# Spare TensorE products of 320 columns, and a shorter chain of VectorE instructions from router logits to gather

## The chip, the cores and the metric

The kernel runs on one core of a Trainium2 chip. The metric is the device time of one execution in microseconds (us), as the median of several runs. A core has a matrix engine (TensorE, in the rows PE, with PEld for its weight loads), VectorE (DVE), ScalarE (ACT), GpSimd (POOL) and a queue engine that issues transfers (SP). They run side by side and meet at semaphores.

## The reference, cut to what matters

Two transformer blocks on 256 tokens of 1024 values, all in float32.

```python
# first block, two layers
for l in range(2):
    x = x + hybrid_mixer(rms_norm(x, norm_mix[l]), ...)
    h = rms_norm(x, norm_ffn[l])
    x = x + (swiglu(h, ...) if l == 0 else moe_swiglu(h, ...))
x = rms_norm(x, norm_final)
# moe_swiglu: 8 experts of width 2816, the two best of each token
logits = h @ router
top_vals, top_idx = top_k(logits, 2); gates = softmax(top_vals)
out = sum over e of gate[:, e] * swiglu(h, wg[e], wu[e], wd[e])
# second block
x = x + attention and short convolution, gated, through w_o
h2 = rms_norm(x)
# hierarchical_moe: the best of 4 groups, then the two best of its 4 experts (width 256)
g = top_1(softmax(h2 @ w_rg + b_rg)); e = top_2(softmax(logits of the experts in the group))
x = x + sum over the chosen of gate * expert(h2)
x = x + sigmoid(rms_norm(x) @ w_pg) * (p @ w_ple)
```

## The kernel before, in words

Each engine has a program of its own, written out by hand in the order of the work (`block.tensor`, `block.vector` and so on), and waits for the others at semaphores; there is no planner. The precision of float32 is kept with two parts: a number is split into a high part in the type fp32r and a low part, the rest, and each product is made three times (high by high, high by low, low by high: `three`, L1033 to L1035).

Weights come as tiles of 1 MB, 128x2048 numbers, into a ring of six slots (`ring`), in one fixed order. For each tile ScalarE writes the high part (`high`, L668; in the expert stages L804), VectorE the low part (`low`, `rest_of`, L1524) into one of three places, and TensorE uses both. SP issues the next transfer into a slot (L500) once the low part of the tile in it is made.

**The norm turns.** `norm(n)` stands on ScalarE and VectorE, `turn(n)` on TensorE. ScalarE squares the first 128 tokens (L676) and so signals `sumsq_ready`, VectorE squares the other 128 (L1537), GpSimd takes the inverse root (L603), VectorE scales both halves (L1548), TensorE turns them in sixteen 128x128 transposes (L1017), ScalarE writes the high part (L684), VectorE the low part (L1524). `norm` on VectorE can be given a weight tile to split after that (`tile`). From `sumsq_ready` on TensorE runs `spare(0, 12)`, twelve 128x128 transposes of the identity into PSUM bank 0 (L1006), whose results nobody reads; the turn after `norm(4)` doesn't exist, since `norm(4)` is not turned.

**The routes.** `route(...)` on TensorE makes the logits with 32 small products (`small_rows`, L1206 and L1207: 16 or 8 columns, in the second block 40 or 20), waits for `exps_wanted`, runs twelve spare transposes into bank 4, waits for `mask_ready`, makes the ranks (ten products, L1220 to L1224), that is for each token and chosen expert how many tokens before it chose the same, and runs sixteen more. On VectorE `route` (first block, L1735 to L1755) and `route2` (second, L1761 to L1791) take the logits, ask ScalarE for the exponentials, find each logit's place among its peers (`places`, L1719 to L1723: five instructions that compare all pairs; `route2` calls it once for the groups and once for the experts of each of four groups), set the mask (L1741; L1772), and make the gates meanwhile. After the ranks they write `table`: for each of three passes (`PASSES`: 96 token slots per expert and pass) three or four instructions. Then comes `over_flag` (L1727 to L1729), three instructions that tell whether any expert has more than 96 tokens, and then the low part of a weight tile.

**The sweep.** `sweeps` waits for the flag's semaphore and calls `sweep`; `choose` copies an expert's row of the table (L1796) and writes the picks, 0/1 matrices of tokens by slots (L1799, L1802). TensorE gathers the chosen tokens with them (`gather_half`, 16 products at L1233 and one transpose at L1235 per half), ScalarE and VectorE split the gathered tokens, and the products of the first expert begin (L1033). After all experts each engine reads the flag and repeats the sweep for the further passes if it is set.

Of the kernel before, what the change touches and what calls it, by code (L numbers as in the profile page):

```python
# [8 lines left out]
ALU = mybir.AluOpType  # L9
# [3 lines left out]
P = 128  # L13
S = 256
TT = S // P
# [3 lines left out]
HALF = 512  # L19
# [6 lines left out]
EXPERTS = 8  # L26
# [3 lines left out]
GROUPS2 = 4  # L30
CAP = 96
PASSES = -(-S // CAP)
# [69 lines left out]
def build(nc, A, out):  # L102
    ctx = ExitStack()
    with ctx:
# [26 lines left out]
        work = sb("work", [P, 5, D])  # L131
# [57 lines left out]
        den = sb("den", [P, 2 + 8])  # L189
        pair_gt, pair_eq = (work[:, 3, k * P:(k + 1) * P] for k in range(2))  # L190
        ntab = (PASSES * EXPERTS) + 1
# [808 lines left out]
        def _(pe):  # L1000
            mm = nc.tensor.matmul

            def spare(b, n):

                for k in range(n):
                    nc.tensor.transpose(PS[:, b, (k % 4) * P:(k % 4 + 1) * P], ident[:], ident[:])  # L1006

            def turn(n):

                if n:  # L1010
                    pe.wait_ge(sumsq_ready, n + 1)
                    spare(0, 12)
                for t in range(TT):
                    pe.wait_ge(norm_applied, 2 * n + t + 1)
                    for b in range(2):
                        for c in range(4):
                            last = nc.tensor.transpose(PS[:, 2 * t + b, c * P:(c + 1) * P],  # L1017
                                                       h[:, t, (4 * b + c) * P:(4 * b + c + 1) * P], ident[:])
                        last.then_inc(h_turned, 1)
# [191 lines left out]
            def route(n, pair, ne, groups, k):  # L1211
# [4 lines left out]
                pe.wait_ge(exps_wanted, k)  # L1216
                spare(4, 12)
                pe.wait_ge(mask_ready, k)
# [5 lines left out]
                mm(PS[:, 1, 2 * groups:3 * groups], ones[:], m[1], start=False, stop=True).then_inc(rank_ready, 1)  # L1224
                spare(4, 16)

# [264 lines left out]
            pe.wait_ge(conv_gated, 2)  # L1491
            spare(4, 8)
            for m in range(4):
# [12 lines left out]
        def _(v):  # L1506
# [224 lines left out]
            def route():  # L1731
# [18 lines left out]
                rank = PS[:, 1, 0:TT * EXPERTS].rearrange("p (t e) -> p e t", t=TT)  # L1750
                for p in range(PASSES):
                    c = slice(p * EXPERTS, (p + 1) * EXPERTS)
                    own.mark(ts(table[:, c, 0, :], rank, float(-p * CAP), None, ALU.add))
                    own.mark(copy(table[:, c, 1, :], m8.rearrange("p t e -> p e t")))
                    own.mark(copy(table[:, c, 2, :], e8.rearrange("p t e -> p e t")))  # L1755
                over_flag(1, EXPERTS)

            def route2():
# [9 lines left out]
                   ALU.subtract).then_inc(exps_wanted, 1)  # L1768
                for g in range(5):
                    places(lg[:, :, 4 * g:4 * g + 4], TT, 4, cnt[:, :, 4 * g:4 * g + 4])  # L1770
                own.link(ts(mk[:, :, 4:20], cnt[:, :, 4:20], 1.5, None, ALU.is_lt))
# [13 lines left out]
                rank = PS[:, 1, 0:TT * GROUPS2].rearrange("p (t e) -> p e t", t=TT)  # L1785
                for p in range(PASSES):
                    c = slice(p * GROUPS2, (p + 1) * GROUPS2)
                    own.mark(ts(table2[:, c, 0, :], rank, float(-p * CAP), None, ALU.add))
                    own.mark(copy(table2[:, c, 1, :], mk[:, :, 0:4].rearrange("p t e -> p e t")))
                    for t in range(TT):  # L1790
                        own.mark(copy(table2[:, c, 2:6, t], ex[:, t, 4:20].rearrange("p (g e) -> p g e", e=4)))  # L1791
                over_flag(2, GROUPS2)

# [88 lines left out]

            def sweep(e, st, s, base, n):
                nc.vector.memset(tick[:, 2:3], 0.0).then_inc(s.added, 1)
                choose(e, s, 0, e.tab[:, base, :, :])
                if not s.base:
                    for k in range(SPLITS):
                        pass_low(e, st, s, 0, k)
                tokens_low(e, s, 0, spread)
                slot_weights(e, s, 0)  # L1890
                choose(e, s, 1, e.tab[:, base + 1, :, :])
                with v.Fori(0, n - 1) as i:
                    experts(e, st, s, i, base, False)
                experts(e, st, s, n - 1, base, True)
                v.wait_ge(s.added, s.n["added"] + 5 * n)

            def sweeps(e, main, rest_s, st_rest, k):
                v.wait_ge(over_ready, k)
                n = e.trips
                sweep(e, stream, main, 0, n)  # L1900
                more = v.value_load(over[0:1, k - 1:k], min_val=0, max_val=1)
# [12 lines left out]
            mixer(1, BASE[2])  # L1914
            norm(3)
            route()
            low(BASE[3] + 2)
            sweeps(moe1, main1, rest1, restream1, 1)
            norm(4, turned=False)
# [143 lines left out]
            add_rows(4, 3, ("o", 3))  # L2063
            norm(6)
            route2()
            low(B + 30)
            sweeps(moe2, main2, rest2, restream2, 2)
            B = BASE[6]
# [26 lines left out]
```

## Time and profile before

| what | us |
|---|---|
| median of 3 runs | 1776.07 |
| the runs | 1776.07, 5672.33, 1775.97 |
| the profiled execution | 1776.7 |
| its span, first to last instruction | 1775.0 |
| TensorE busy | 1671.7 (94% of the span) |
| VectorE busy | 1285.5 (72%) |
| ScalarE busy | 1008.4 (57%) |
| mean granted TensorE clock | 0.965 of full |

The span is what lies between the first and the last instruction of the program in the one profiled execution; its own time is 1.7 us longer. TensorE's clock is granted at one of two levels, 1.2 or 2.4 GHz; the column PEclk gives the mean over a stretch, 1.00 being 2.4 GHz and 0.50 being 1.2 GHz. Matmuls overlap, so the length of one is more than the step from one to the next; the step comes from a stretch's length and its count. One run of the three lies far from the other two, and the median is not moved by it.

### The profile page before, as it was taken

To read this page: it belongs to the slowest core of one execution; us is meant where nothing else is said; L and a number is where in the kernel's file an instruction comes from. 1 tells how busy PE (TensorE), PEld (TensorE's weight loads), DVE (VectorE), ACT (ScalarE), POOL (GpSimd) and SP (SyncE) were. 2 spreads that over 40 slices of the span, in tenths; PEclk is the share of its full clock that TensorE was granted. 3 is DMA by queue.
4 is the path that set the end of the run, shared out by engine and by line. 5 is a ranking of instruction groups with operands and counts; after the bars stand their busy time and mean duration, and the time that the engine had idled before them with its cause. 6 is when DMAs were issued, how large, how long until landed. Compare 5 with 4: busy or idle time off the path is not lost.

```text
span 1775.0 us, 23849 instructions
## 1 busy us (share of the span) xinstructions
PE 1671.7 (94%) x9475; PEld 1357.1 (76%) x9475; DVE 1285.5 (72%) x1152; ACT 1008.4 (57%) x861; POOL 23.1 (1%) x37
## 2 busy tenths in 40 slices
PE   6989999897999999999999999999789999799997
PEld 6969999896777776767777676777588798788875
DVE  5984444796687888888787888888657545577764
ACT  4744334464476767767676767767444353266653
POOL 3000000000000000000000000000000000000000
PEclk9999999998899999999999999999979799799999
DMA  9535555433497989899798989989744334368860
GB/s 285 188 121 177 188 184 188 149 102 119 177 372 290 366 314 357 304 351 386 284 379 306 360 298 355 373 299 369 257 141 127 124 120 143 107 230 286 286 241 25
DMA packets 240762, 431.54 MB, mean 243 GB/s; under 512 B 11540, under 2 KB 121648, under 8 KB 240688
## 3 DMA queue, kind: packets, MB, share of 16 engines
q1 hardware_dynamic: 239200, 426.17, 68.8%
q10 hardware_dynamic: 1488, 4.34, 0.7%
q8 instruction: 51, 0.84, 0.2%
q14 instruction: 23, 0.19, 0.0%
HBM read 429.44 MB, written 1.05 MB: 243 GB/s over the span
## 4 chain that ended last, share of the span: by engine, by line
PE 75%; issue 14%; DVE 7%; ACT 3%; DMA 1%; POOL 0%; DVEq 0%; SPq 0%; POOLq 0%; ACTq 0%
PE PS L1033 22%; PE PS L1035 22%; PE PS L1034 22%; PE PS L1113 2%; DVE w_low L1524 2%; PE PS L1247 2%; PE PS L1279 1%; ACT w_high L804 1%; DVE hT_low L1524 1%; PE PS L1408 1%; ACT w_high L668 1%; PE PS L1407 1%; DVE h L1548 1%; DMA ring<-in_w_in_dram 1%; PE PS L1206 0%
## 5 line engine op out<-in xcount | busy, mean ns | idle before, releaser
L1524 DVE TENSOR_TENSOR w_low<-ring,w_high 128x2048 fp32r<-128x2048 f32 x402 | 917.4, 2289 | 321.0 <-ACT w_high L668 172.1
L804 ACT ACTIVATE w_high<-ring 128x2048 fp32r<-128x2048 f32 x306 | 585.5, 1918 | 270.6 <-PE PS L1035 270.4
L1033 PE MATMUL PS<-w_high,hT_high 128*96 128x512 f32 (+3 forms) x1184 | 421.0, 356 | 12.3 <-DVE hT_low L1524 7.3
L1035 PE MATMUL PS<-w_high,hT_low 128*96 128x512 f32 (+3 forms) x1184 | 413.4, 349 | 0.0
L1034 PE MATMUL PS<-w_low,hT_high 128*96 128x512 f32 (+3 forms) x1184 | 412.0, 348 | 0.0
L668 ACT ACTIVATE w_high<-ring 128x2048 fp32r<-128x2048 f32 x96 | 182.9, 1910 | 143.3 <-PE PS L1035 139.5
L1033 PE MATMUL PS<-hT_high,w_high 128*128 128x256 f32 x832 | 242.1, 291 | 8.2 <-DVE hT_low L1524 6.4
L1033 PEld LDWEIGHTS PS<-w_high,hT_high 128*96 128x96 f32 (+1 forms) x1184 | 196.6, 166 | 63.8 <-DVE hT_low L1524 8.0
L1034 PE MATMUL PS<-hT_low,w_high 128*128 128x256 f32 x832 | 239.1, 287 | 0.0
L1035 PE MATMUL PS<-hT_high,w_low 128*128 128x256 f32 x832 | 238.9, 287 | 0.0
L1033 PE MATMUL PS<-w_high,yT_high 128*96 128x512 f32 (+1 forms) x568 | 228.0, 401 | 8.2 <-DVE yT_low L1524 8.2
L1034 PEld LDWEIGHTS PS<-w_low,hT_high 128*96 128x96 f32 (+1 forms) x1184 | 196.9, 166 | 48.6 <-issue 2.7
L1035 PEld LDWEIGHTS PS<-w_high,hT_low 128*96 128x96 f32 (+1 forms) x1184 | 196.7, 166 | 47.8
L1035 PE MATMUL PS<-w_high,yT_low 128*96 128x512 f32 (+1 forms) x568 | 224.2, 395 | 0.0
L1034 PE MATMUL PS<-w_low,yT_high 128*96 128x512 f32 (+1 forms) x568 | 223.8, 394 | 0.0
L1033 PEld LDWEIGHTS PS<-hT_high,w_high 128*128 128x128 f32 x832 | 163.6, 197 | 11.2 <-DVE hT_low L1524 7.2
L1034 PEld LDWEIGHTS PS<-hT_low,w_high 128*128 128x128 f32 x832 | 163.5, 197 | 0.9 <-issue 0.5
L1035 PEld LDWEIGHTS PS<-hT_high,w_low 128*128 128x128 f32 x832 | 163.4, 196 | 0.0
L1033 PEld LDWEIGHTS PS<-w_high,yT_high 128*96 128x96 f32 (+1 forms) x568 | 96.7, 170 | 44.3 <-DVE yT_low L1524 9.7
L1035 PEld LDWEIGHTS PS<-w_high,yT_low 128*96 128x96 f32 (+1 forms) x568 | 96.5, 170 | 35.8
L1034 PEld LDWEIGHTS PS<-w_low,yT_high 128*96 128x96 f32 (+1 forms) x568 | 96.9, 171 | 34.8 <-issue 1.0
L1814 DVE TENSOR_TENSOR x_res<-x_res,PS 128x512 f32<-128x512 f32 x48 | 33.0, 687 | 30.0 <-PE PS L1247 30.0
(289 smaller groups left out, 1306.7 us busy)
## 6 DMA issues: line engine op xcount, KB each, us to landing
ring<-in_moe_wg_dram SPq DMA_DIRECT2D x88, 1024.0 KB, 6.6
ring<-in_moe_wu_dram SPq DMA_DIRECT2D x88, 1024.0 KB, 7.0
ring<-in_moe_wd_dram SPq DMA_DIRECT2D x80, 1024.0 KB, 6.3
ring<-in_w_in_dram SPq DMA_DIRECT2D x36, 1024.0 KB, 5.6
ring<-in_w_gate_dram SPq DMA_DIRECT2D x16, 1024.0 KB, 6.4
ring<-in_w_up_dram SPq DMA_DIRECT2D x16, 1024.0 KB, 6.1
ring<-in_w_down_dram SPq DMA_DIRECT2D x16, 1024.0 KB, 5.9
ring<-in_ffn_wg_dram SPq DMA_DIRECT2D x11, 1024.0 KB, 5.4
```

The source lines that it names most:

```text
L668: act.activation(w_high[:, T % SPLITS, :], slot(w), ACT.Copy).then_inc(split_high, 1)
L804: act.activation(w_high[:, (s.base + k) % SPLITS, :], slot(w), ACT.Copy).then_inc(s.high_taken, 1)
L1033: mm(o, left_high, right_high, start=first, stop=False, skip_group_check=shared)
L1034: mm(o, left_high, right_low, start=False, stop=False, skip_group_check=shared)
L1035: return mm(o, left_low, right_high, start=False, stop=last_one, skip_group_check=shared)
L1113: last = mm(chunks(1 if c == 3 else 3, 1)[:, 0, :], diag[:, 8 * (m % 2) + k - k0, :], cpad[:, c, k:k + S], start=(k == 0), stop=(k == (TAP ...
L1247: mm(bank((6 + hf, 1 + 2 * hf)[t]), spread[0:CAP, t * P:(t + 1) * P], wk[4][0:CAP, hf * HALF:(hf + 1) * HALF], start=True, stop=True).then ...
L1279: last = nc.tensor.transpose(PS[:, 6 + j % 2, c * CAP:(c + 1) * CAP], wk[2 + j % 2][0:CAP, c * P:(c + 1) * P], ident[0:CAP, 0:CAP])
L1407: mm(o, qz[:, hd, t * P:(t + 1) * P], uT[:, hd // 2, 0:n], start=True, stop=False)
L1408: last = mm(o, head_row[0:HEADS, hd, :], negc[:, 0:n], start=False, stop=True)
L1524: return tt(out_, whole, part.bitcast(F32), ALU.subtract)
L1814: tt(o, o, bank((6 + hf, 1 + 2 * hf)[t]), ALU.add).then_inc(s.added, 1)
```

## The change: longer spare products, and steps of VectorE taken out or moved

On TensorE, `spare` now multiplies the split router table of the second block with its own first 128 columns: 128 rows, 320 columns, fp32r, one product each. `spare_turns` is the old transpose and is left for turn 1, where the table isn't made yet. The counts change: turn 1 from 12 to 28 transposes; turns 2, 3, 5, 6 and 7 from 12 transposes to 20 products; turn 5 gets 20 more behind a wait for the squares of `norm(4)`; the routes from 12 and 16 transposes to 14 and 8 products (first) and 6 and 8 (second); before the rows of `w_o` from 8 transposes to 6 products.

On VectorE, `route2` calls `places` once for all 20 logits of both token halves (its scratch grows to 160 numbers, so its two buffers lie 512 apart); both routes write only the first pass of the table before the gather, and return a function `later` with the other passes and the overflow flag, which `sweep` calls after the first `choose`; the wait for the flag moves behind the sweep; and the low part of the weight tile moves from after the route into the norm before it.

```diff
-        pair_gt, pair_eq = (work[:, 3, k * P:(k + 1) * P] for k in range(2))
+        pair_gt, pair_eq = (work[:, 3, k * HALF:(k + 1) * HALF] for k in range(2))
...
+            idle = router2_pair[:].rearrange("p c n -> p (c n)")
             def spare(b, n):
+                for k in range(n):
+                    mm(PS[:, b, 0:320], idle[:, 0:P], idle, start=True, stop=True)
+            def spare_turns(b, n):
                 for k in range(n):
                     nc.tensor.transpose(PS[:, b, (k % 4) * P:(k % 4 + 1) * P], ident[:], ident[:])
             def turn(n):
+                if n == 5:
+                    pe.wait_ge(sumsq_ready, 5)
+                    spare(0, 20)
                 if n:
                     pe.wait_ge(sumsq_ready, n + 1)
-                    spare(0, 12)
+                    if n == 1:
+                        spare_turns(0, 28)
+                    else:
+                        spare(0, 20)
...
                 pe.wait_ge(exps_wanted, k)
-                spare(4, 12)
+                spare(4, (14, 6)[k - 1])
                 pe.wait_ge(mask_ready, k)
...
-                spare(4, 16)
+                spare(4, 8)
...
             pe.wait_ge(conv_gated, 2)
-            spare(4, 8)
+            spare(4, 6)
...
-                for p in range(PASSES):
-                    c = slice(p * EXPERTS, (p + 1) * EXPERTS)
-                    own.mark(ts(table[:, c, 0, :], rank, float(-p * CAP), None, ALU.add))
-                    own.mark(copy(table[:, c, 1, :], m8.rearrange("p t e -> p e t")))
-                    own.mark(copy(table[:, c, 2, :], e8.rearrange("p t e -> p e t")))
-                over_flag(1, EXPERTS)
+                def passes(first, n):
+                    for p in range(first, n):
+                        c = slice(p * EXPERTS, (p + 1) * EXPERTS)
+                        own.mark(ts(table[:, c, 0, :], rank, float(-p * CAP), None, ALU.add))
+                        own.mark(copy(table[:, c, 1, :], m8.rearrange("p t e -> p e t")))
+                        own.mark(copy(table[:, c, 2, :], e8.rearrange("p t e -> p e t")))
+                    own.settle()
+                def later():
+                    passes(1, PASSES)
+                    over_flag(1, EXPERTS)
+                passes(0, 1)
+                return later
...
-                for g in range(5):
-                    places(lg[:, :, 4 * g:4 * g + 4], TT, 4, cnt[:, :, 4 * g:4 * g + 4])
+                places(lg[:].rearrange("p t (g e) -> p (t g) e", e=4), TT * 5, 4,
+                       cnt[:].rearrange("p t (g e) -> p (t g) e", e=4))
...
-            def sweep(e, st, s, base, n):
+            def sweep(e, st, s, base, n, later=None):
                 nc.vector.memset(tick[:, 2:3], 0.0).then_inc(s.added, 1)
                 choose(e, s, 0, e.tab[:, base, :, :])
+                if later:
+                    later()
...
-            def sweeps(e, main, rest_s, st_rest, k):
+            def sweeps(e, main, rest_s, st_rest, k, later):
+                n = e.trips
+                sweep(e, stream, main, 0, n, later)
                 v.wait_ge(over_ready, k)
-                n = e.trips
-                sweep(e, stream, main, 0, n)
...
-            norm(3)
-            route()
-            low(BASE[3] + 2)
-            sweeps(moe1, main1, rest1, restream1, 1)
+            norm(3, tile=BASE[3] + 2)
+            later = route()
+            sweeps(moe1, main1, rest1, restream1, 1, later)
...
-            norm(6)
-            route2()
-            low(B + 30)
-            sweeps(moe2, main2, rest2, restream2, 2)
+            norm(6, tile=B + 30)
+            later = route2()
+            sweeps(moe2, main2, rest2, restream2, 2, later)
```

`route2` is split into `passes` and `later` in the same way as `route`.

## Rows read from the trace of the kernel before

**Rows 1.** Windows: stretch, length, busy of PE, PEld, DVE, ACT, POOL; PEclk, DMA, GB/s.
```profile
431.40:458.70 27.30, 23.73 (x109) 22.84 (x110) 10.76 (x39) 5.48 (x8) 0.00 (x0) 0.50 0.24 77
458.70:1281.30 822.60, 806.85 (x3843) 577.06 (x3842) 682.47 (x466) 570.46 (x394) 0.00 (x0) 1.00 0.92 333
...
1520.30:1530.50 10.20, 5.49 (x44) 4.78 (x44) 7.31 (x10) 5.72 (x8) 0.70 (x1) 1.00 0.47 153
1530.50:1550.90 20.40, 15.98 (x73) 15.08 (x73) 10.84 (x57) 0.68 (x2) 0.00 (x0) 0.50 0.15 50
```

**Rows 2.** Waits, 460 to 1275 us: in total, times, longest; the longest of all.
```profile
ACT w_high L804 <- PE PS L1035: 223.0, 234, 4.3
```

**Rows 3.** Windows in which TensorE has no gap: 512 columns, 512 columns, 256 columns.
```profile
1500.50:1518.50 18.00, 18.00 (x81) 14.85 (x80) 6.48 (x3) 5.75 (x3) 0.00 (x0) 1.00 0.57 174
1496.40:1499.40 3.00, 3.00 (x7) 2.40 (x8) 2.43 (x2) 1.62 (x1) 0.00 (x0) 0.50 0.00 0
1330.00:1340.00 10.00, 10.00 (x86) 10.00 (x85) 4.58 (x2) 4.43 (x3) 0.00 (x0) 1.00 0.62 201
```

**Rows 4.** Timeline of TensorE, turns 1, 2 and 7: start, us, instruction, [idle before].
```profile
125.52 2.29 PE L1017 MATMUL PS<-ident,h 128*128 128x128 f32 x16 [2.81 <-DVE h L1548]
...
319.14 2.82 PE L1006 MATMUL PS<-ident 128*128 128x128 f32 x12 [2.50 <-ACT h L676]
...
322.66 0.86 PEld L1017 LDWEIGHTS PS<-ident,h 128*128 128x128 f32 x8 [1.09 <-DVE h L1548]
...
1738.87 2.29 PE L1017 MATMUL PS<-ident,h 128*128 128x128 f32 x16 [0.84 <-DVE h L1548]
```

**Rows 5.** Timeline of turn 3 and route 1, to the first expert product.
```profile
426.00 1.53 PE L1006 MATMUL PS<-ident 128*128 128x128 f32 x12 [0.76 <-ACT h L676]
...
434.68 0.38 PE L1206 MATMUL PS<-router_pair,hT_high 128*128 128x16 f32 x1 [1.41 <-DVE hT_low L1524]
...
441.70 0.17 DVE L1735 COPY lg<-PS 128x16 f32<-128x16 f32 x1 [7.08 <-PE PS L1207]
...
442.55 2.82 PE L1006 MATMUL PS<-ident 128*128 128x128 f32 x12 [0.89 <-DVE shifted L1738]
...
443.91 0.17 DVE L1741 TENSOR_SCALAR mk<-cnt 128x16 f32<-128x16 f32 x1
...
444.95 0.55 PEld L1220 LDWEIGHTS PS<-mk,above 128*128 128x128 f32 x2
...
447.42 0.17 DVE L1753 TENSOR_SCALAR table<-PS 128x16 f32<-128x16 f32 x1 [2.51 <-PE PS L1224]
...
448.59 2.27 DVE L1524 TENSOR_TENSOR w_low<-ring,w_high 128x2048 fp32r<-128x2048 f32 x1
450.79 0.15 DVE L1796 COPY now<-table 128x6 f32<-128x6 f32 x1
...
452.08 3.73 PE L1233 MATMUL PS<-uT,h 128*128 128x96 f32 x16 [1.27 <-DVE uT L1802]
...
460.58 0.47 PE L1033 MATMUL PS<-w_high,hT_high 128*96 128x512 f32 x1 [1.36 <-DVE hT_low L1524]
```

**Rows 6.** Timeline of route 2, from the first small product to the gather's second half.
```profile
1528.73 0.29 PE L1206 MATMUL PS<-router_pair,hT_high 128*128 128x40 f32 x1 [1.57 <-DVE hT_low L1524]
...
1534.22 0.20 DVE L1761 TENSOR_TENSOR lg<-PS,bias 128x40 f32<-128x40 f32 x1 [5.55 <-PE PS L1207]
...
1540.23 0.17 DVE L1772 TENSOR_SCALAR mk<-cnt 128x8 f32<-128x8 f32 x1
...
1542.86 0.17 DVE L1788 TENSOR_SCALAR table<-PS 128x8 f32<-128x8 f32 x1 [0.98 <-PE PS L1224]
...
1546.42 0.16 DVE L1796 COPY now<-table 128x12 f32<-128x12 f32 x1
...
1547.24 3.73 PE L1233 MATMUL PS<-uT,h 128*128 128x96 f32 x16 [0.97 <-DVE uT L1799]
...
1550.96 1.92 PE L1233 MATMUL PS<-uT,h 128*128 128x96 f32 x16
```

More of the change, by code:

```diff
@@ L1785, in route2, with passes, later @@
                 rank = PS[:, 1, 0:TT * GROUPS2].rearrange("p (t e) -> p e t", t=TT)
[L1786 to L1792, printed above, removed]
+                def passes(first, n):
+                    for p in range(first, n):
+                        c = slice(p * GROUPS2, (p + 1) * GROUPS2)
+                        own.mark(ts(table2[:, c, 0, :], rank, float(-p * CAP), None, ALU.add))
+                        own.mark(copy(table2[:, c, 1, :], mk[:, :, 0:4].rearrange("p t e -> p e t")))
+                        for t in range(TT):
+                            own.mark(copy(table2[:, c, 2:6, t], ex[:, t, 4:20].rearrange("p (g e) -> p g e", e=4)))
+                    own.settle()
+                def later():
+                    passes(1, PASSES)
+                    over_flag(2, GROUPS2)
+                passes(0, 1)
+                return later
             def choose(e, s, i, src):
```

## The prediction, on record before the changed kernel was run

> **What bounds the kernel now.** I read the stretches of granted clock first, then the waits of the expert stage, then two timelines. The expert stage of the first block is one long stretch at 2.4 GHz in which TensorE is busy 806.85 of 822.6 us [rows 1]; in it ScalarE and VectorE wait for TensorE and for one another, and no wait for a weight transfer is listed [rows 2]. So TensorE carries the end, and what is won ahead of an expert stage arrives there whole. What isn't TensorE's peak lies between the stages: from 431.4 to 458.7 us and from 1530.5 to 1550.9 us the engine is granted half its clock, 1.2 GHz, around the two routers, and in both it waits for chains of short VectorE instructions. The change works on these two places and on the six norm turns where spare products run.
>
> **Price of a spare product.** The trace has no 128x320 product. At 2.4 GHz, 81 products of 512 columns fill 18.0 us (0.222 each), 86 of 256 columns fill 10.0 (0.116); at 1.2 GHz 7 of 512 fill 3.0 (0.43) [rows 3]. Between 0.116 and 0.222 at full clock, I take the share of columns: 320/512 x 0.222 = 0.14, and 0.27 at the low clock. Twenty are 2.8 to 2.9 us or 5.4 us; twelve transposes now take 1.3 to 1.5 or 2.8 us [rows 4].
>
> **The turns.** Spare work costs nothing while it ends before the normalized rows come. In turn 1 the cover is 1.53 + 2.81 = 4.3 us [rows 4]; 28 transposes at 0.86/8 = 0.108 are 3.0: no cost (at the low clock 6.0, so +1.7). In turn 2 the spares start at 319.14 at the low clock (2.82 us for twelve) and the rows come at 322.66, a cover of 3.5 us [rows 4]. The clock rose by then, so of twenty products about 3.0 us run at 0.27 (eleven) and nine at 0.14: 4.3 us, +0.8 us; bounds 0 and +1.9. Turns 3 and 6 start at full clock (twelve transposes in 1.53 us [rows 5]; 1520.3 to 1530.5 is at full clock [rows 1]): 2.9 is inside the cover of turn 1's size, 0. Turn 7 covers only 1.53 + 0.84 = 2.4 us [rows 4], so the transposes come 0.5 late, but VectorE has a weight tile's 2.3 us to do before it takes them: 0, bounds 0 and +3. Turn 5 gets one more group while TensorE would only wait for the norm before; it ends before the next, and another weight tile stands on VectorE ahead of the turned rows: 0, bounds -1.7 and +1. The two spares fewer before the `o` rows: 0.
>
> **Route 1.** It takes 34.6 us from spares (426.00) to the first expert product (460.58) [rows 5]. I take it in five steps.
> (a) Turn and logits. Now the clock falls at 431.4 [rows 1], in the second half of the transposes, after twelve spares and an idle time. With twenty products the engine is busier there, so I take the course of route 2, where the turn ran at full clock and the clock fell half way through the 32 small products. There, first small product to logits takes 1534.22 - 1528.73 = 5.5 us; here 441.70 - 434.68 = 7.0 [rows 5, 6]: -1.5, and the transposes at full clock -0.7. Together -2.2; bounds 0 and -4.2 (all 32 at full clock).
> (b) Logits to ranks. The spares start 0.85 after the logits (442.55), the mask is ready 2.4 after (444.1), the ranks' first weights load at 444.95, 3.25 after. Fourteen products at the low clock last 3.8, so the ranks start 0.85 + 3.8 = 4.65 after: +1.4. At full clock 2.9: -0.3. I take +1.3. Behind them on TensorE stand ranks, eight spares and gather.
> (c) Ranks to table: 447.42 - 444.95 = 2.5 us at the low clock, half of it at full clock. In turn 2 the clock came back after twelve transposes at the low one, and fourteen products are somewhat more work, so it may be back here; I take half the chance: -0.5.
> (d) Table to gather: 447.42 to 452.08 is 4.7 us. Three passes of three instructions and three of the overflow flag fill 447.42 to 448.59, the tile's low part what is left to 450.79, the picks the rest. The first pass (0.3), a wait for it (0.1) and the picks (1.3) stay: 1.7, so -3.0. The low part moves under the small products, where VectorE waits for the logits: no cost, and the slot's next transfer is issued earlier. The passes and the flag move under the gather's first half (at least 1.9 us against 0.9): no cost; if that cover were gone, +1. The eight spares (2.1 at worst) end as the picks are ready.
> (e) Gather to first expert product: 460.58 - 452.08 = 8.5 us, 32 products at the low clock. Route 2's second half shows the full clock: sixteen from 1550.96 in 1.92 us, against 3.73 for the first [rows 6]. One half sooner is -1.8, both -3.5; I take -2.6.
> Sum: -2.2 + 1.3 - 0.5 - 3.0 - 2.6 = -7.0 us, bounds -1.6 (the clock low from the turn on) and -12.2 (full all through).
>
> **Route 2.** Logits to mask is 1540.23 - 1534.22 = 6.0 us with five calls of `places`; route 1 with one call takes 443.91 - 441.70 = 2.2. One more threshold (0.2) and 160 elements for 128 in five steps and 40 for 16 in four (0.3) make 2.7: -3.3. The six spares (0.95 + 1.6 = 2.55) end before it. Table to gather is 1547.24 - 1542.86 = 4.4; first pass 0.45 and 1547.24 - 1546.42 = 0.8 stay: -3.1. Now TensorE would be late: eight spares behind the ranks at the low clock last 2.1 and hold the gather 0.4: +0.4. Less idle time before the gather brings the clock back sooner in it: -0.4, bounds 0 and -1.6. Sum -6.4; bounds -5 and -10.7 (all at full clock).
>
> **The transposes and the clock.** After twelve spare transposes at 1.2 GHz, turn 2's own transposes ran at 0.108 us, full clock [rows 4], so here transposes do bring it back. The Trainium skill ("TensorE: Matmul & The Clock Gate", Part 4: PE-mode transpose) says the full clock does not engage for transposes because they don't count as busy in the same way. By it the products would do at each place what transposes could not, and the sum would be that of the full-clock rival; by the row they only add some weight, and the sum stands. The trace disagrees with the rule.
>
> **Sum.** +0.8 - 7.0 - 6.4 = -12.6 us. The profiled execution took 1776.7 us (1775.0 of it the span); 1776.7 - 12.6 = 1764.1, and the median shown, 1776.07, lies 0.6 lower: 1763.5.
>
> **Rivals.**
> *Full clock throughout.* The spares keep 2.4 GHz from turn to gather. Route 1: -4.2 - 0.3 - 1.2 - 3.0 - 3.5 = -12.2; route 2: logits -1.9, places -3.3, ranks -0.7, table -3.1, gather -1.6 = -10.6. 1753.3. For it: twenty products last twice as long as twelve transposes (2.9 against 1.3). Against: in route 2 the clock fell after a turn at full clock [rows 1, 6], and the 32 small products between are unchanged.
> *Low clock as now.* Only VectorE's steps are won. Route 1: +1.4 - 3.0 = -1.6; route 2: -3.3 - 3.1 + 0.4 = -6.0; turn 2 +0.8: -6.8, 1769.3. For it: fourteen products may be too few.
> *The weight stream takes route 1's gain.* The experts start earlier and meet unlanded tiles: -12.6 + 7.0 = -5.6, 1770.5. For it: DMA 0.92 busy in that stage [rows 1]. Against: no such wait in [rows 2], and the ring is full by then.
> *Slower: spares at the low clock outlast their cover.* If the clock has fallen before each turn, twenty last 5.4 us against covers of 3.5 to 4.3 (turns 2, 3 and 6: +1.9, +1.5, +1.5) and 2.4 (turn 7: +3.0), route 1's ranks wait +1.4, route 2's gather +0.4, and the transposes of two turns and route 2's logits run low (+1.4, +1.5): 12.6 against 3.0 + 3.3 + 3.1 = 9.4 won, +3.2: 1779.3. It decides once three of the four turns start low. Against: only turn 2 starts low now.
>
> **Chances.** Forecast 0.58, full clock 0.17, low clock 0.15, stream 0.04, slower 0.06. The clock's steps move with the code, so each case has two or three microseconds around it. From 1756 to 1770 the range holds the forecast, the low clock and an edge of the full clock, about 8 in 10. Two per cent, about what a measurement of this kernel tells from no change, is 35 us; no case reaches it. Faster 0.01, same 0.98, slower 0.01.
>
> **What would show it.** Right: five VectorE instructions of `places` in route 2 instead of 25; 1.7 and 1.3 us from table to gather; small products of route 1 that start at full clock and slow down; the gathers mostly at full clock; in turn 2 transposes that follow the last spare with no idle time. Wrong: a low stretch of 27 us at route 1 as now, none at all, or ScalarE waiting for the ring early in the expert stage.

## The result, and the profile after

The changed kernel took 1760.82 us, the median of 4 runs (1760.31 to 1765.53), beside 1776.89 for the kernel before in the same comparison (again with one run of 5672.33 among its four): a ratio of 0.9914, with a 95% interval from 0.9896 to 0.9932. That is 12 to 18 us less. The forecast was 12.6 us less, 1763.5. A second comparison of the same code, x0 below, gave 1762.15 and 0.9924 [0.9903, 0.9945].

The page of the changed kernel: busy times, and TensorE's clock in forty slices.

```profile
span 1758.6 us, 23939 instructions
PE 1670.0 (95%) x9529; PEld 1360.7 (77%) x9529; DVE 1283.3 (73%) x1132; ACT 1007.7 (57%) x861; POOL 24.6 (1%) x37
PEclk9999999999999999999999999999989899899999
```

TensorE is busy as long as before (1671.7 then), with other work in the gaps; the span is 16.4 us shorter. Windows of the changed kernel, cut where the clock changes (columns as in [rows 1]):

```profile
427.00:438.00 11.00, 7.64 (x50) 6.32 (x48) 8.68 (x11) 4.95 (x7) 0.70 (x1) 1.00 0.54 205
438.00:448.30 10.30, 9.41 (x41) 9.33 (x42) 5.11 (x15) 1.68 (x3) 0.00 (x0) 0.50 0.49 178
448.30:1277.70 829.40, 812.85 (x3892) 582.79 (x3890) 685.81 (x486) 570.94 (x395) 0.00 (x0) 1.00 0.91 330
...
1510.00:1523.50 13.50, 10.14 (x66) 8.57 (x64) 11.43 (x13) 6.04 (x8) 0.70 (x1) 1.00 0.44 149
1523.50:1537.10 13.60, 12.62 (x55) 12.12 (x55) 7.45 (x37) 0.60 (x2) 0.00 (x0) 0.50 0.22 78
```

The low stretch of route 1 is 10.3 us, where [rows 1] have 27.3, and that of route 2 is 13.6 for 20.4. The expert stage looks as it did, and the ring isn't late in it: of its waits, 450 to 1270 us, the first is again ScalarE's for TensorE, 223.1 us as in [rows 2].

```profile
ACT w_high L804 <- PE PS L1048: 223.1, 234, 4.3
```

The timeline of the changed kernel, turns 1 and 2 (answers to [rows 4]):

```profile
123.06 4.95 PE L1013 MATMUL PS<-ident 128*128 128x128 f32 x28 [2.18 <-ACT h L676]
127.84 1.91 PE L1030 MATMUL PS<-ident,h 128*128 128x128 f32 x16
...
321.46 4.73 PE L1008 MATMUL PS<-router_pair 128*128 128x320 f32 x20 [2.49 <-ACT h L676]
326.03 1.91 PE L1030 MATMUL PS<-ident,h 128*128 128x128 f32 x16
```

Neither row of the turn's own transposes (L1030) has an idle time in brackets: in both turns the spares ended last, and the normalized rows waited for them. Turn 3 and route 1 (answers to [rows 5]):

```profile
429.32 3.19 PE L1008 MATMUL PS<-router_pair 128*128 128x320 f32 x20 [0.80 <-ACT h L676]
...
437.27 0.28 PE L1219 MATMUL PS<-router_pair,hT_high 128*128 128x16 f32 x1 [1.57 <-DVE hT_low L1537]
...
438.21 2.29 DVE L1537 TENSOR_TENSOR w_low<-ring,w_high 128x2048 fp32r<-128x2048 f32 x1 [1.00 <-ACT w_high L668]
...
443.62 0.17 DVE L1748 COPY lg<-PS 128x16 f32<-128x16 f32 x1 [3.12 <-PE PS L1220]
444.47 4.02 PE L1008 MATMUL PS<-router_pair 128*128 128x320 f32 x14 [0.89 <-DVE shifted L1751]
...
448.33 0.28 PE L1233 MATMUL PS<-mk,above 128*128 128x8 f32 x2
...
449.62 0.17 DVE L1768 TENSOR_SCALAR table<-PS 128x16 f32<-128x16 f32 x1 [2.79 <-PE PS L1237]
450.00 0.17 DVE L1827 COPY now<-table 128x6 f32<-128x6 f32 x1
451.16 0.17 DVE L1768 TENSOR_SCALAR table<-PS 128x16 f32<-128x16 f32 x1
451.30 2.02 PE L1246 MATMUL PS<-uT,h 128*128 128x96 f32 x16 [0.52 <-DVE uT L1833]
...
456.67 0.47 PE L1046 MATMUL PS<-w_high,hT_high 128*96 128x512 f32 x1 [1.37 <-DVE hT_low L1537]
```

The low part of the weight tile (438.21) now stands in VectorE's wait for the logits, and the second pass of the table (451.16) in its wait for the gather. Route 2 (answers to [rows 6]):

```profile
1527.06 0.20 DVE L1783 TENSOR_TENSOR lg<-PS,bias 128x40 f32<-128x40 f32 x1 [2.17 <-PE PS L1220]
1527.87 0.32 DVE L1732 TENSOR_TENSOR work<-lg 128x160 f32<-128x160 f32 x1
...
1529.75 0.17 DVE L1794 TENSOR_SCALAR mk<-cnt 128x8 f32<-128x8 f32 x1
...
1532.13 2.48 PE L1008 MATMUL PS<-router_pair 128*128 128x320 f32 x8
1532.38 0.17 DVE L1812 TENSOR_SCALAR table<-PS 128x8 f32<-128x8 f32 x1 [0.98 <-PE PS L1237]
...
1533.03 0.57 DVE L1830 TENSOR_SCALAR uT<-slot_no,now 128x96 f32<-128x96 f32 x2
...
1534.41 3.22 PE L1246 MATMUL PS<-uT,h 128*128 128x96 f32 x16
1537.57 1.92 PE L1246 MATMUL PS<-uT,h 128*128 128x96 f32 x16
```

The picks are ready at 1533.6, but the eight spares in front of the gather go on to 1534.4, and the gather starts with no idle time. One comparison of 160 elements took 0.32 us.

**Where the time went.** From the same marks in both traces (the start of a norm's squares on ScalarE, the first product after a turn, the first expert product):

| stretch | before | after | difference | forecast |
|---|---|---|---|---|
| start to the squares of turn 1 | 119.98 | 121.86 | +1.9 | none |
| turn 1, squares to next product | 9.40 | 9.79 | +0.4 | 0 |
| turn 2, the same | 8.58 | 9.57 | +1.0 | +0.8 |
| squares of turn 3 to first expert product | 35.79 | 28.55 | -7.2 | -7.0 |
| expert stage 1, and turn 5 | 837.5 | 837.5 | 0 | 0 |
| after turn 5 to the squares of turn 6 | 222.0 | 218.8 | -3.2 | none |
| squares of turn 6 to first expert product | 34.37 | 28.07 | -6.3 | -6.4 |
| expert stage 2, turn 7, tail | 220.6 | 217.6 | -3.0 | 0 |

The stretches left out differ by under 0.1. The rows that the change touches sum to -12.1, with turn 1, for a forecast of -12.6. Three others differ as well (+1.9, -3.2, -3.0). In the attention stage, after turn 5, the kernel before had places of low clock at 1298.4, 1387.1 and 1404.2 (37.5 us in all), the changed one at 1294.8, 1383.5 and 1404.0 (30.6 us). TensorE never pauses in the two of them shown here, and has half its clock all the same; first the kernel before, then the changed one.

```profile
1404.20:1421.20 17.00, 17.00 (x48) 10.50 (x48) 6.68 (x11) 4.45 (x17) 0.00 (x0) 0.50 0.17 62
```

```profile
1404.00:1414.20 10.20, 10.20 (x36) 7.61 (x36) 5.68 (x10) 0.73 (x1) 0.00 (x0) 0.50 0.15 59
```

The 6.9 us less at half speed are the -3.2. (x0 to x11 are the experiments below.) With a further place that both have at the stage's end (3.4 us, from 1496.4 and from 1489.4) the kernel before has 41.0 us of low clock there and the changed one 34.1. Over the ten profiles with the small products and the spares of one of these two kernels, or eight spares more, the stage's time goes with that sum: 216.6 to 217.3 us with 30 to 31 us of it (x1, x5, x10), 218.2 to 218.9 with 34 (changed, x2, x3, x11), 221.3 to 222.0 with 41 (before, x0, x6). That the difference isn't the change's is shown by x0, the same code again: 221.3 us for this stretch, while x2 and x5, with turn 5 and attention as in the kernel before, took 218.2 and 216.6.

The last row goes the same way: its part up to the squares of turn 7 took 179.4 us where no place of low clock stood in it (changed, x3, x6, x9), 180.8 to 181.0 with one of 3.4 us (before and four others), 182.4 to 182.5 with two (x0 and three others). The +1.9 of the first row is not the clock's: the changed kernel has no low clock up to 121.86, the kernel before has 6.8 us of it and is there sooner. Over all profiles this stretch took 119.98 to 121.89 us; why is open. In x0 the first row of the table was +0.5 and the last +1.7, for +1.9 and -3.0 here. The kernel before spread from 1766.55 to 1782.0 us over 31 runs of one comparison (one more took 3689.82), so a single pair of profiles isn't good for the last few microseconds; the ratios are.

### The profile page after: what moved, and what is told of

It reads as the page before. It is cut to its first block, busy times and chain, and to the rows that moved or that the text cites. A ratio compares the mean times of both kernels' runs of the same rounds, so it can differ in the third digit from the quotient of the medians.

```text
span 1758.6 us, 23939 instructions
## 1 busy us (share of the span) xinstructions
PE 1670.0 (95%) x9529; PEld 1360.7 (77%) x9529; DVE 1283.3 (73%) x1132; ACT 1007.7 (57%) x861; POOL 24.6 (1%) x37
## 4 chain that ended last, share of the span: by engine, by line
PE 85%; DVE 8%; ACT 3%; issue 2%; DMA 1%; DVEq 0%; POOL 0%; SPq 0%; ACTq 0%
PE PS L1046 25%; PE PS L1048 25%; PE PS L1047 24%; DVE w_low L1537 3%; PE PS L1260 2%; PE PS L1126 2%; ACT w_high L804 1%; PE PS L1292 1%; DVE hT_low L1537 1%; PE PS L1008 1%; ACT w_high L668 1%; DMA ring<-in_w_in_dram 1%; PE PS L1421 1%; PE PS L1420 1%; PE PS L1219 1%
## 5 line engine op out<-in xcount | busy, mean ns | idle before, releaser
L1048 PE MATMUL PS<-w_high,yT_low 128*96 128x512 f32 (+1 forms) x568 | 223.1, 393 | 0.0
```

Of the source, the lines that this page charges most:

```text
L1048: return mm(o, left_low, right_high, start=False, stop=last_one, skip_group_check=shared)
```

## The experiments

The theory going in is the prediction's: 9.4 us from VectorE's shorter chain, and the rest, net of what the spares cost, from a clock that the longer spares hold up. The main rivals: the products do something that transposes can't; or the spares give nothing. Three groups of kernels ran, each beside the kernel before on the same chip (its medians: 1776.18, 1775.81 and 1775.31 us).

**x1: the products alone.** The kernel before with the new `spare` and its new counts; VectorE as before.

```diff
-                    spare(0, 12)
+                    if n == 1:
+                        spare_turns(0, 28)
+                    else:
+                        spare(0, 20)
...
-                spare(4, 16)
+                spare(4, 8)
```

> The kernel before with all edits of TensorE's program (the products and their counts) and none of VectorE's. Theory (clock and chain both pay): the small gain of the clock in gather and ranks of route 1 (3 to 6 us), less the ranks that wait for fourteen products there (1.3) and for turns 1 and 2 (1 to 3): 1771 to 1777 us. Rival (the products pay nothing, all comes from VectorE's shorter chain): 1777 to 1780, since only their price is left. Rival (the products pay most): under 1769.

Measured: 1771.64 us, 0.9980 [0.9963, 0.9998], some 3.6 us won; squares to first expert product 33.48 in route 1 (-2.3) and 34.40 in route 2 (0). The clock's part, taken alone, stands nearly all in route 1. Less the +0.4 and +1.0 of turns 1 and 2, which x1 pays too, the places of the change show only 0.9 us in this profile; the rest of its 4.2 us comes from the attention stage (217.3 for 222.0) and the start (121.45 for 119.98), which both move without the change as well.

**x2: VectorE alone.** The changed kernel with the old transposes and counts on TensorE.

```diff
-                    if n == 1:
-                        spare_turns(0, 28)
-                    else:
-                        spare(0, 20)
+                    spare(0, 12)
...
-                spare(4, (14, 6)[k - 1])
+                spare(4, 12)
...
-                spare(4, 8)
+                spare(4, 16)
```

> The changed kernel with the spare work of before (twelve and sixteen transposes, nothing before norm 5): VectorE's edits alone. Theory: 3.0 us in route 1 and 3.3 + 3.1 in route 2, less what sixteen transposes behind the ranks (3.4 us at 1.2 GHz) now hold of the gather, 1 to 2 us in each route: 1767 to 1770 us. Rival (all comes from here): 1760 to 1762. Rival (the chain wasn't on the path): 1775 or more.

Measured: 1764.61 us, 0.9954 [0.9932, 0.9976], some 8.2 us won, which is 1768 by the ratio and inside what was expected; the median itself lies 2.4 us under it, and its twelve runs spread from 1759.63 to 1774.28. In the profiled one, which is among the fastest (1760.49), the routes took 31.59 (-4.2) and 27.30 (-7.1). With x1's, the parts sum to -6.5 and -7.1, for -7.2 and -6.3 of both together. TensorE's timeline of x2, route 1, and its windows of low clock in both routes:

```profile
447.40 3.65 PE L1006 MATMUL PS<-ident 128*128 128x128 f32 x16
450.84 2.49 PE L1233 MATMUL PS<-uT,h 128*128 128x96 f32 x16
```

```profile
431.50:452.00 20.50, 18.16 (x84) 17.68 (x85) 10.28 (x37) 5.11 (x7) 0.00 (x0) 0.50 0.32 103
1523.80:1534.00 10.20, 9.21 (x45) 9.12 (x45) 6.61 (x37) 0.24 (x1) 0.00 (x0) 0.50 0.28 103
```

The picks' chain begins at 448.03, but the sixteen old transposes hold the gather to 450.84, 2.8 us later, where eight products leave 1.3. So a shorter chain needs its spares cut with it. And the low stretch of route 1 begins at 431.5, as before, since the turn has its twelve transposes again.

**x3: transposes of as many columns.** The changed kernel, with five 128-column transposes for every four products of 320.

```diff
-                for k in range(n):
-                    mm(PS[:, b, 0:320], idle[:, 0:P], idle, start=True, stop=True)
+                for k in range(-(-n * 5 // 4)):
+                    nc.tensor.transpose(PS[:, b, (k % 4) * P:(k % 4 + 1) * P], ident[:], ident[:])
```

> The changed kernel with each group of 320-column products replaced by transposes of the identity for the same number of columns at the same rate (20 products by 25 transposes, 14 by 18, 8 by 10, 6 by 8). Theory (transposes raise the clock as products do, as the trace of before showed in turn 2): within 2 us of the changed kernel, 1759 to 1763. Rival (the Trainium skill, TensorE: Matmul & The Clock Gate, Part 4: transposes don't count as busy): the clock stays low around both routes and in the turns, 1766 or more, and more low stretches than the eleven of before.

Measured: 1760.58 us, 0.9922 [0.9899, 0.9945]: the same as the changed kernel. TensorE's timeline of x3, turn 2 and before the ranks of route 1:

```profile
320.13 4.62 PE L1008 MATMUL PS<-ident 128*128 128x128 f32 x25 [2.50 <-ACT h L676]
324.58 1.91 PE L1030 MATMUL PS<-ident,h 128*128 128x128 f32 x16
...
442.98 3.92 PE L1008 MATMUL PS<-ident 128*128 128x128 f32 x18 [0.88 <-DVE shifted L1751]
446.75 0.29 PE L1233 MATMUL PS<-mk,above 128*128 128x8 f32 x2
```

The clock was low from 320.3 to 323.7 and came back while the transposes ran, as it does in the changed kernel's twenty products; at the full clock throughout, in turn 3, the same 25 took 2.89 us. Without the last one, at the very end of the program, x3's stretches of low clock sum to 78.5 us, as much as the changed kernel's. What kind the spares are makes no difference that these intervals could show. That speaks against the rule of the Trainium skill ("TensorE: Matmul & The Clock Gate", Part 4: PE-mode transpose) that the full clock doesn't engage for transposes, which the prediction weighed, and for the row that it went by.

**x4: no spares at all.** VectorE as changed, `spare` and `spare_turns` emit nothing.

> The changed kernel with no spare work at all. Theory: nothing waits for spares any more (2 us in turn 1, 1 in turn 2, 1.3 in route 1's ranks, all of them won back), but the clock is low through turns, routes and gathers and in the first products after each turn, 1.7 to 3.4 us at each of seven places: 1765 to 1772 us. Rival (the spares cost as much as they give): 1758 to 1762. Rival (they are what carries the gain): 1775 or more.

Measured: 1773.01 us, 0.9991 [0.9971, 1.0011]: about all of the gain is gone, more than expected, nearer to the rival. Windows of x4 at route 1, behind turn 5 and at route 2:

```profile
433.30:457.20 23.90, 17.36 (x79) 16.83 (x80) 12.20 (x39) 6.16 (x8) 0.00 (x0) 0.50 0.26 88
1283.20:1310.50 27.30, 16.54 (x76) 16.17 (x77) 19.70 (x28) 13.18 (x15) 1.39 (x2) 0.50 0.38 113
1528.90:1546.00 17.10, 12.68 (x60) 12.52 (x60) 8.45 (x39) 1.34 (x3) 0.00 (x0) 0.50 0.18 62
```

Without spares in turn 5 the clock stays low for 27.3 us, where the changed kernel has 6.8 and 10.2. But the marks of the table don't put the loss there: 14.4 of the 27.3 us are turn 5 itself, which took 14.35 us as in both kernels, and the attention stage after it took 219.7 us, for 218.8 and 221.3 of the two profiles of the changed kernel. The loss stands in the routes: 32.7 us in route 1 (28.6 and 28.4) and 30.6 in route 2 (28.1 and 26.4), that is 6.7 to 8.5 us of the 8.9 to 11.4 by which this profile is longer than those two. With the same VectorE work, no spares stand at 0.9991, the old ones (x2) at 0.9954 and the new ones at 0.9914 and 0.9924. Spares as such are worth 12 to 14 us, and the change's counts 5 to 7 of them over the old ones. That last figure is the less certain: the intervals of x2 and x3 overlap, x1 had 3.6 us for the same edits, and a part of it isn't clock but the eight spares fewer in front of the gather. Which of the changed counts it hangs on wasn't taken apart, but for the two groups of x10.

**x0: the changed kernel again.** 

> The changed kernel once more, word for word, with more runs. The steps of the clock fall differently in each execution, so its runs should spread over some 8 us as those of the other kernels did. Theory: a ratio to before of 0.991 to 0.994 and a median of 1759 to 1765 us; in the profile route 1 (squares of norm 3 to first expert product) 27 to 31 us and route 2 26 to 29. Rival (part of the first measured gain was a lucky position of the clock's steps): 0.994 or more.

Measured: 1762.15 us, 0.9924 [0.9903, 0.9945], inside what was expected. The spread was not: its six runs lie within 2.1 us (1760.7 to 1762.81), for the 8 expected. In its profile route 1 took 28.4 us and route 2 26.4, and turns 1 and 2 took 9.37 and 8.58 us, as in the kernel before: in this execution no place of low clock stood in them, and the longer spares cost nothing.

**x5: `places` alone.** The kernel before with one call of `places` in `route2`.

> The kernel before with places called once in route 2 and nothing else. Theory: 3.3 us, a ratio of 0.9975 to 0.9985, with logits to mask 2.7 us in the profile. Rival (the chain wasn't what the ranks waited for): ratio 0.9995 or more.

Measured: 1771.84 us, 0.9978 [0.9958, 0.9998], some 3.9 us; from logits to mask 2.69 us for 6.01.

**x11: table and low part alone.** x2 with the five calls of `places` back.

> The kernel before with only the table's later passes, the flag and the low part moved: no places at once and no products. Theory: 3.0 and 3.1 us less what sixteen transposes (3.4 us at 1.2 GHz) hold of the gather, 1.0 to 1.8 in each route: 2.5 to 4.5 us, 1771.5 to 1773.5; in the profile the gather starts with no idle time behind the last transpose. Rival (the gather is free to start): 6 us.

Measured: 1769.54 us, 0.9973 [0.9954, 0.9992], some 4.8 us. A little over the expected gain. In the profile the gather follows the last transpose with no idle time in both routes, as expected. With x5's 3.9 it makes 8.7, for 8.2 of x2: the parts add up within their intervals.

**x6: the gap behind the transposes filled.** Eight more products after the transposes of turns 2, 3, 5, 6 and 7.

```diff
                         last.then_inc(h_turned, 1)
+                if n > 1:
+                    spare(4, 8)
```

> The changed kernel with eight more products behind the transposes of turns 2, 3, 5, 6 and 7, where TensorE waits for the low parts (1.4 to 1.9 us idle, in turns 5 and 7 3.5 or more). Theory (what brings the clock down in the routes is the small products, not this gap): within 2 us of the changed kernel, and the low stretches in both routes remain. Rival (the gap decides): the clock stays high into the small products and beyond, 3 to 5 us faster.

Measured: 1762.3 us, 0.9927 [0.9906, 0.9948]: nothing, beside x0. From squares to logits 15.4 and 14.2 us, for 15.5 and 14.1.

**x7: x6, and a product after each pair of small ones.**

```diff
+                        if (t, c) != (TT - 1, KC - 1):
+                            spare(4, 1)
```

> As the one before, and one 320-column product after each pair of small products, at routes 1 and 2 and at the small products behind turn 5 (15 each). At full clock a call of 32 small products with them is 3.4 + 15 x 0.148 = 5.6 us against 5.4 to 6.9 with the clock low for part of them. Theory (the small products let the clock fall): no low stretch from turn to gather in either route nor behind turn 5, logits at most 0.5 us later or up to 1 sooner, ranks and gather wholly at full clock, and 3 us won behind turn 5: 4 to 7 us faster than the changed kernel. Rival (32 small products hold the clock low whatever stands among them): the low stretches remain and it is 5 us or more slower.

Measured: 1768.67 us, 0.9956 [0.9940, 0.9972], some 6 us more than x0, where 4 to 7 less were expected; it is the rival that came. The theory missed what it does behind turn 5, where the attention stage took 225.0 us (x0: 221.3), and in route 2, which took 31.9 (26.4). Windows of x7, up to route 1's logits, behind turn 5, and route 2:

```profile
427.80:441.50 13.70, 11.46 (x86) 10.62 (x85) 8.78 (x17) 5.48 (x7) 0.69 (x1) 1.00 0.54 177
1291.50:1305.20 13.70, 13.70 (x63) 13.70 (x62) 5.04 (x8) 3.33 (x5) 0.00 (x0) 0.50 0.44 139
1527.00:1544.10 17.10, 16.11 (x70) 15.61 (x70) 6.56 (x37) 0.24 (x1) 0.00 (x0) 0.50 0.19 61
```

In route 1 the clock held until 441.5, behind the logits, and they still came 6.0 us after the first small product (6.35 in the changed kernel), because the fifteen products stand in the chain; then it fell for 3.4 us. In route 2 it fell, and the logits took 8.7 us (5.4). Work that is put between needed work has to buy more than its own time, and here it doesn't.

**x8: the router as the stationary operand.** x7 says that the small products themselves are what is to be made shorter. Each loads 128 columns of tokens to multiply 8 to 40 columns of router. Turned round, 16 products of 256 token columns do it, ScalarE copies the logits out of PSUM, and two small transposes turn them back.

```diff
+            def small_cols(o, pair, n):
+                for c in range(KC):
+                    mm(o[0:2 * n, :], pair[:, c, :], hT_high[:, c, :], start=(c == 0), stop=False, skip_group_check=True)
+                    last = mm(o[0:n, :], pair[:, c, 0:n], hT_low[:, c, :], start=False, stop=(c == KC - 1),
...
-                small_rows(PS[:, 0, 0:4 * ne], pair, ne).then_inc(logits_ready, 1)
+                small_cols(PS[:, 2, 0:S], pair, ne)
+                spare(4, 4)
+                small_turned(PS[:, 0, 0:4 * ne], ne, (1, 3)[k - 1]).then_inc(logits_ready, 1)
...
-                spare(4, (14, 6)[k - 1])
+                spare(4, (8, 8)[k - 1])
```

It is used in both routes and for the eight columns behind turn 5.

> The changed kernel with the operands of the small products changed over at both routes and behind turn 5: the router table is the stationary side (16, 8, 40 or 20 columns) and 256 tokens move, 16 products of 256 columns for 32 of 8 to 40; ScalarE copies the turned logits out, TensorE turns them back in two transposes. Four spare products cover the copy, and eight instead of fourteen and six stand before the ranks. Theory (32 products of a few columns are slow, 0.106 us each whatever their width, and are what lets the clock fall): 16 x 0.12 = 1.9 us, the copy 0.8 and the transposes 0.5, so logits 3.2 to 3.6 us after the first product against 5.4 to 6.9; the clock high through both gathers and behind turn 5: 5 to 9 us faster than the changed kernel, 1753 to 1757. Rival (the clock falls anyway in the wait for the copy): 1 to 3 us faster. Rival (the copy waits on ScalarE behind weight tiles or a table load): no gain.

Measured: 1748.20 us, 0.9850 [0.9827, 0.9873]: 27 us less than the kernel before, some 13 less than the changed one, and more than the 5 to 9 that were expected. The timeline of x8 in route 1, and its window:

```profile
436.79 0.29 PE L1236 MATMUL PS<-hT_high,router_pair 128*16 128x256 f32 x1 [1.57 <-DVE hT_low L1566]
...
438.65 0.75 PE L1017 MATMUL PS<-router_pair 128*128 128x320 f32 x4
438.85 0.37 ACT L876 ACTIVATE lgT<-PS 16x256 f32<-16x256 f32 x1 [1.15 <-PE PS L1237]
439.33 0.29 PE L1245 MATMUL PS<-ident,lgT 16*128 16x16 f32 x2
439.94 0.17 DVE L1777 COPY lg<-PS 128x16 f32<-128x16 f32 x1
```

```profile
436.60:450.80 14.20, 10.83 (x82) 9.42 (x82) 9.19 (x39) 4.76 (x7) 0.00 (x0) 1.00 0.42 143
```

The logits are there 3.15 us after the first product, for 6.35, and the whole of route 1 runs at 2.4 GHz. Squares to first expert product is 24.4 and 25.7 us (28.55 and 28.07), and after turn 5 to the squares of turn 6 is 210.8 (218.8). So x8 wins 4.1, 2.4 and 8.1 us over the changed kernel by its profile, of which the last holds the luck of one execution too: this stage has 20.5 us of low clock for 34.1. In route 2 the clock still falls, at 1514.3, for 6.8 us. The turned operands, the four spares over the copy and the new counts before the ranks came in together; what each is worth wasn't measured.

**x9: x8 with fewer spares.** 12 transposes in turn 1, no group ahead of turn 5, and x6's eight products behind the transposes.

> As the one before, with twelve transposes in turn 1 instead of 28, no products before norm 5, and eight more products behind the transposes of turns 2, 3, 5, 6 and 7. Theory (28 transposes only cost where the clock falls among them, the group before norm 5 does nothing, and the gap filled holds the clock once the small products are broad): 1 to 3 us faster than the one before. Rival (each spare group pays by itself): slower than the one before.

Measured: 1748.62 us, 0.9850 [0.9828, 0.9873]: no different from x8; the further gain that was expected isn't there.

**x10: the changed kernel without two groups.** 12 transposes in turn 1 for 28, and no twenty products behind the squares of `norm(4)`.

> The changed kernel with twelve transposes in turn 1 and without the twenty products before norm 5. Theory: 0 to 2 us faster, since turn 1 now paid 0.4 us at its own place in the profile and the group before norm 5 changed nothing between the squares and the first product after it. Rival (they hold the clock for what follows): 2 us or more slower.

Measured: 1761.23 us, 0.9923 [0.9903, 0.9944], as x0: those two groups neither pay nor cost as far as these intervals show.

## Why the prediction was right

The sum held: 12.6 us less forecast, 13.5 (x0) and 15.3 (first comparison) measured by the ratios, each with the forecast inside its interval. Point by point:

- *Price of a spare.* 0.14 and 0.27 us were expected. Twenty at 2.4 GHz, in turn 3, took 3.19 us with the last one's tail, so somewhat under 0.16 each (their weight loads fill 2.93 us, 0.147 each); fourteen at the low clock spanned 444.47 to 448.33, 0.276 each. Right.
- *Turns.* Turn 2's twenty products took 4.6 us to the first transpose, for 4.3, the clock being low from 322.0 to 325.4: +1.0 for +0.8. Turn 1 is the step that went the other way: its 28 transposes were costed at full clock, 3.0 us inside a cover of 4.3. In the profiled execution the clock fell at 124.0, among them, and they took 4.8. The cost was +0.4 of the bound's +1.7. It isn't the count alone: x5 and x10, with twelve transposes in turn 1 and the clock falling there as well, took 10.4 us for this turn (9.4 without the fall, in the kernel before and in x0, which has the 28). Turn 2's +1.0 is of the same kind, and absent in x0. Turn 7's twenty took 4.65 us at the low clock, and the product after them came 0.14 us later: the 0 held.
- *Route 1.* (a) -1.5 us for the logits' products was -0.7, since the clock fell at 438.0, after 0.7 us of small products, where route 2's in [rows 6] had 1.8; the transposes' -0.7 was -0.7. (b) Logits to ranks, +1.3, was +1.2. (c) -0.5 was -1.0: the fourteen products brought the clock back at 448.3, and the ranks ran at 2.4 GHz. (d) -3.0 was -3.0, 1.68 us from table to gather. (e) -2.6 was -3.1, both gather halves at the full clock. The clock's terms missed in both directions by up to 0.8 and cancelled, which is luck.
- *Route 2.* Logits to mask 2.69 us for a forecast of 2.7. Table to gather 2.03, a gain of 2.35 for 2.7: the spares at the low clock held the gather 0.8 us, not 0.4. Gather and after -0.56 for -0.4.
- *Rivals.* "Full clock throughout" didn't come: two low stretches stand in the routes. "Low clock as now" is excluded by route 1's 10.3 us. The weight stream took nothing, 223.1 us of ScalarE waiting for TensorE as before. "Spares outlast their cover" is what turns 1 and 2 show, at +1.4 together, far from the price at which it decides. "The products can do what transposes can't" is refuted by x3.

What the prediction didn't have is the weight of the old spares. It took the clock's part as what the longer ones add. x4 shows that spares altogether carry 12 us or more, by its profile mostly in the two routes; turn 5's additional group, costed at 0, is worth nothing that x10 could show.

## What to carry to other kernels

When a chain on another engine is made shorter, count again the spare work that was sized to its old length: it becomes the wait. Before filling the gaps around a run of small products, look at what one of them costs; with the narrow operand made the stationary one, half as many products did the same work here, with less low clock around them. And where the length of the low stretches differs from execution to execution, compare stages over several profiles: one pair showed a 3.2 us gain in a stage that the change leaves alone.

## What the runs showed of the hardware

- Transposes of fp32 data raise and hold TensorE's clock as fp32r products of as many columns do, within the intervals (x3: 0.9922 for 0.9914 and 0.9924, and the same 78.5 us of low clock).
- The clock also falls where TensorE has no pause: 17.0 busy of 17.0 us at 1.2 GHz in the attention stage, and 10.1 of 10.1 us (1377.0 to 1387.1) before the fall at 1387.1. Where it falls there isn't chance: in all fourteen profiles it does so twice, while the attention logits are made or just behind them (before: 1387.1 and 1404.2; x8: 1374.3 and 1394.7), and the low stretches then last from 3.4 to 17 us. Half of these products have 8 rows, as in the line below, from the kernel before; that this is the cause wasn't tested.

```profile
1409.48 1.22 PE L1408 MATMUL PS<-spread,head_row 8*128 8x256 f32 x2
```

- x7 held the clock up to route 1's logits and lost it among route 2's small products, with the same products in the same order but for their width (16 and 8 columns, 40 and 20). What settles it was not found.
- A small product's time doesn't follow its columns: those of 16 and 8 columns in route 1 follow each other at 0.11 us at 2.4 GHz and 0.21 at 1.2, and a product of 256 columns in x8 takes no longer (16 of them from 436.79 to 438.65, 0.116 each).
- One VectorE comparison of 160 elements took 0.32 us, and one of the table's copies 0.17: few, wide instructions (five for 25) are what made `places` 3.3 us shorter.
